# A conditioned transformer pair on one core: x loaded behind the second weight chunk and transposed one value group later

## The reference

```python
def rms_norm(x, g):
    y = x * rsqrt(mean(x * x, axis=-1) + 1e-6) * g

mod = silu(c) @ w_ada + b_ada                       # 1024 -> 3 * 1024
shift, scale, gate = split(mod, 3)
h = rms_norm(x, g_pre) * (1.0 + scale) + shift      # 512 x 1024, block 1's input
proj = h @ w_in                                     # queries, keys, values, gates of block 1
...                                                 # two attentions, output projection
x = x + gate * rms_norm(y, g_post)

mem_h = rms_norm_2(mem, mem_norm_g)                 # 256 x 1024
k, v = split(mem_h @ w_mem_kv, 2)                   # block 2's memory: keys, values
k = rms_norm_2(k per head of 256, kn_g)
...                                                 # block 2: convolution, two attentions, merge
```

## Time and profile before

| | us |
|---|---|
| runs (3): median | 1176.51 |
| lowest, highest | 1174.89, 1177.65 |
| the profiled execution: its own time | 1176.51 |
| the profiled execution: span from first to last instruction | 1174.7 |
| TensorE busy | 1141.0 |
| VectorE busy | 815.1 |
| ScalarE busy | 586.9 |
| mean granted clock of TensorE | 0.996 |

### The profile page before, as it was taken

The page is one execution under the profiler, slowest core; times in us unless marked ns, Lnnn a source line. Parts: engine busy times, 40 slices in busy tenths (PEclk is TensorE's granted clock), DMA queues, the critical chain, the costliest instruction groups (busy, mean ns, idle before and its releaser), DMA issues.

```text
span 1174.7 us, 16788 instructions
## 1 busy us (share of the span) xinstructions
PE 1141.0 (97%) x6375; PEld 948.0 (81%) x6380; DVE 815.1 (69%) x1352; ACT 586.9 (50%) x1064; POOL 64.2 (5%) x73
## 2 busy tenths in 40 slices
PE   5899999999999999999999999999999999999998
PEld 5899777766899977777777778888888888788898
DVE  5788555668575237888898885898788686853351
ACT  5663455456564455766657655324554223651320
POOL 1029400101000000000000000000000000000000
PEclk9899999999999999999999999999999999999999
DMA  9967222321454322212222143232222323223221
GB/s 343 345 223 273 91 72 73 90 63 37 148 180 157 108 72 72 72 37 90 72 90 73 36 144 126 72 108 90 90 73 84 132 81 109 97 73 108 104 85 46
DMA packets 36208, 130.41 MB, mean 111 GB/s; under 512 B 4272, under 2 KB 6576, under 8 KB 35616
## 3 DMA queue, kind: packets, MB, share of 16 engines
q1 hardware_dynamic: 32560, 112.74, 29.0%
q0 software_dynamic: 3280, 16.29, 4.2%
q10 hardware_dynamic: 288, 0.31, 0.1%
HBM read 121.72 MB, written 6.29 MB: 109 GB/s over the span
## 4 chain that ended last, share of the span: by engine, by line
PE 87%; DVE 6%; ACT 3%; issue 2%; DMA 2%; SPq 0%; POOL 0%; DVEq 0%; ACTq 0%
PE bank L463 26%; PE bank L465 25%; PE bank L464 25%; PE bank L529 2%; PE bank L677 2%; DMA raw<-in_chunks 2%; DVE wl L1760 1%; PE bank L800 1%; PE bank L705 1%; PE bank L631 1%; ACT qf L1164 1%; DVE ca L2173 1%; DVE stat L1915 0%; PE bank L807 0%; DVE cumt L2441 0%
## 5 line engine op out<-in xcount | busy, mean ns | idle before, releaser
L463 PE MATMUL bank<-hl,wh 128*128 128x512 f32 x888 | 361.7, 407 | 0.9 <-DVE u L2187 0.9
L465 PE MATMUL bank<-hh,wh 128*128 128x512 f32 x888 | 347.1, 391 | 0.0
L464 PE MATMUL bank<-hh,wl 128*128 128x512 f32 x888 | 346.2, 390 | 0.0
L1102 ACT ACTIVATE wh<-raw 128x1024 fp32r<-128x1024 f32 x185 | 191.1, 1057 | 188.9 <-PE bank L465 178.1
L1760 DVE TENSOR_TENSOR wl<-raw,wh 128x1024 fp32r<-128x1024 f32 x185 | 225.2, 1242 | 84.5 <-ACT wh L1102 84.1
L463 PEld LDWEIGHTS bank<-hl,wh 128*128 128x128 f32 x888 | 167.2, 188 | 37.9 <-issue 4.8
L465 PEld LDWEIGHTS bank<-hh,wh 128*128 128x128 f32 x888 | 166.6, 188 | 36.4
L464 PEld LDWEIGHTS bank<-hh,wl 128*128 128x128 f32 x888 | 167.3, 188 | 33.6 <-issue 3.1
L2173 DVE SCALAR_TENSOR_TENSOR ca<-u,vt,ca 128x512 f32<-128x512 f32 x232 | 157.9, 745 | 0.0
L464 PE MATMUL bank<-oh,wl 128*128 128x512 f32 (+1 forms) x256 | 93.9, 367 | 0.0
L465 PE MATMUL bank<-oh,wh 128*128 128x512 f32 (+1 forms) x256 | 93.9, 367 | 0.0
(11 more groups left out here) (323 smaller groups left out, 1676.2 us busy)
## 6 DMA issues: line engine op xcount, KB each, us to landing
raw<-in_chunks SPq DMA_DIRECT2D x193, 512.0 KB, 3.7
ada_a<-in_chunks SPq DMA_DIRECT2D x8, 512.0 KB, 10.9
ada_b<-in_chunks SPq DMA_DIRECT2D x8, 512.0 KB, 8.6
x<-in_x POOLq DMA_DIRECT2D x4, 512.0 KB, 10.5
mem_scratch<-kvm POOLq DMA_DIRECT2D x1, 2048.0 KB, 8.2
x<-in_x POOLq DMA_DIRECT2D x1, 2048.0 KB, 8.1
x_scratch<-x POOLq DMA_DIRECT2D x1, 2048.0 KB, 7.7
kvm<-mem_scratch POOLq DMA_DIRECT2D x1, 2048.0 KB, 9.5
```

Of the source, the lines that this page charges most:

```text
L463: pe.matmul(o, a[0], b[1], start=start, stop=False, **kw)
L464: pe.matmul(o, a[1], b[0], start=False, stop=False, **kw)
L465: return pe.matmul(o, a[0], b[0], start=False, stop=stop, **kw)
L1102: act.activation(wh[:, SLOT[nxt]], raw[:, RAW_SLOT[nxt]], ACT.Copy).then_inc(s.w_hi, 1)
```

## The change

Five edits, all in the first stage.

1. **Load of x.** GpSimd's queue waits until `mk1` has landed before it issues x (and the small vectors behind it).
2. **Order of pieces.** `ADA_BEHIND` puts `mk2` straight behind `mk1`, ahead of the first two ada pieces; `mk3` gets three pieces behind it. From `mk4` on the list is as before.
3. **Memory's squares.** ScalarE squares the memory's first tile only; VectorE squares and sums the second (`tensor_tensor_reduce`, with `macc` as a scratch output) ahead of its scaling of the packed vectors. A new signal, `mem_squared`, joins the two ahead of the root.
4. **x's squares and normalisation.** ScalarE squares x and takes the root at the end of head 2 and no longer ahead of head 0; the hi copy of `mk3` moves behind head 0's squares and copy. VectorE scales x into `xn` at the end of head 3, where it stood at the end of head 0.
5. **Transposes of x.** They stand ahead of value groups 1 and 2, where they stood ahead of 0 and 1.

```diff
-ADA_BEHIND = (0, 2, 1, 2, 1, 1, 1, 1, 1, 1, 1, 1, 2, 1, 0, 0, 0, 2, 0, 2, 0, 2, 0, 2)
+ADA_BEHIND = (0, 0, 2, 3, 1, 1, 1, 1, 1, 1, 1, 1, 2, 1, 0, 0, 0, 2, 0, 2, 0, 2, 0, 2)
...
             for g in range(4):
-                if g < 2:
-                    if g == 0:
+                if g in (1, 2):
+                    if g == 1:
                         pe.wait_ge(s.xn_done, 4)
-                    to_features(xn, "xT", range(4 * g, 4 * g + 4))
+                    to_features(xn, "xT", range(4 * g - 4, 4 * g))
...
         def _(pool):
+            wait_raw(pool, ("mk", 1))
             for tt in range(T):
                 pool.dma_start(x[:, tt, :], t["x"][0, tt * P:tt * P + P, :]).then_inc(s.x_in, 16)
...
-            square_rows(memx, MEM_SS, 2)
-            act.wait_ge(s.sumsq, 2)
+            square_rows(memx, MEM_SS, 1)
+            act.wait_ge(s.sumsq, 1)
+            act.wait_ge(s.mem_squared, 1)
...
-            ahead(None)
-            act.wait_ge(s.x_in, 16 * T)
-            square_rows(x, X_SS, T)
-            act.wait_ge(s.sumsq, 6)
-            act.activation(X_SS, X_SS, ACT.Sqrt, scale=1.0 / D, bias=eps6).then_inc(s.small_sqrt, 1)
+            ahead(None, 3)
...
+                if h == 0:
+                    ahead(None)
                 ahead(("mk", 2 * h + 1))
+                if h == 2:
+                    act.wait_ge(s.x_in, 16 * T)
+                    square_rows(x, X_SS, T)
+                    act.wait_ge(s.sumsq, 5)
+                    act.activation(X_SS, X_SS, ACT.Sqrt, scale=1.0 / D, bias=eps6).then_inc(s.small_sqrt, 1)
             for g in range(4):
-                if g < 2:
-                    x_copies(g)
+                if g in (1, 2):
+                    x_copies(g - 1)
...
+            dve.wait_ge(s.mem_in, 16 * 2)
+            dve.tensor_tensor_reduce(macc[:, 0, :], memx[:, 1, :], memx[:, 1, :], 1.0, 0.0, ALU.mult, ALU.add,
+                                     MEM_SS[:, 1:2]).then_inc(s.mem_squared, 1)
             dve.wait_ge(s.rows_in, 16)
...
                 ahead(("mk", 2 * h + 1))
-                if h == 0:
+                if h == 3:
                     dve.wait_ge(s.small_sqrt, 2)
                     then(dve.reciprocal(X_SS, X_SS))
```

More of the change, by code:

```diff
@@ L146 @@
     "tables_in": "masks, distances, slopes and blocks loaded",
-    "mem_in": "memory loaded", "x_in": "x loaded", "bcast_in": "lambdas and sinks loaded on every partition", "late_in": "positions, gate bias and gain",
+    "mem_in": "memory loaded", "mem_squared": "squares of the memory's second tile added up", "x_in": "x loaded", "bcast_in": "lambdas and sinks loaded on every partition", "late_in": "positions, gate bias and gain",
     "swapped": "halves of heads swapped for the rotation", "wmask_in": "banded masks of two tiles loaded", "sel_in": "rows that pick a head's bias loaded",
@@ L1079, in out_parts @@
             return [((kind, g, half), 2 * half + i, 256 * i) for i in range(2)]
-        squared_at = {name: 6 + 2 * n + 2 for n, name in enumerate(SQUARED)}
+        squared_at = {name: 5 + 2 * n + 2 for n, name in enumerate(SQUARED)}
         @block.scalar
@@ L1416, in out_squares @@
                     banks.wait_full(act, key)
-                    if squares[0] > 6:
+                    if squares[0] > 5:
                         act.wait_ge(s.sumsq, squares[0])
```

## The result

The changed kernel takes 1181.16 us (median of 5 runs, 1180.81 to 1182.37) against 1176.71 for the kernel before (median of 5, 1174.89 to 1177.84). The ratio is 1.0042, 95% interval 1.0031 to 1.0054: **4.5 us slower**. 1180.9 us had been forecast. The profiled execution took 1181.8 us, with a span of 1180.0, 5.3 more than before.

What follows compares the result with a forecast made beforehand. TensorE, busy 97% of the span, was taken as the bound. Start nothing, the 7.0 us key lead lost in x's chain: +2.1, plus +2.3 for half clock, +4.4 on 1176.51: 1180.9 us, range 1177.0 to 1184.5.

Steps and rivals of the forecast that it cites:

- Part 3: x's squares, root and scaling: chain from `mv1`'s load makes TensorE wait 8.4 us for `xn`; at full pace 2.1 us lost.
- Part 4: TensorE around the wait for `xn`: half clock costs 2.3 us, bounds 0 and 4.2.
- Part 1: Start of the first stage: gain of 0 to 3 us at first transposes, worth nothing by itself; `mk4` runs at 29.85.
- a sign of being right: TensorE's `mk4` matmuls start at 29 to 31 us and head 1's sums end near 36.5.
- a start away from 30: Sign of being wrong: `mk4` starting well away from 30 us would mean the loads don't come by bytes alone.
- Part 2: Keys on TensorE: head 1's sums end at 36.46, not 43.47, a lead of 7.0 us.
- Rival B: Wait for `xn` costs no clock, so only 2.1 us are lost: 1178.6 us; chance 0.12.
- A: At x's transposes: the lead reaches the end, `mod` 6.2 us earlier, 1170.3 us; break-even with `xn` by 56.7; chance 0.05.
- C: Half clock at both TensorE waits (`mk4`, `xn`) and through x's transposes: 2.1 + 2.1 + 4.2, 1184.9 us; chance 0.11.

Runs made afterwards that it cites:

- e2: Kernel before with edits 1 to 3 alone; x's squares, scaling and transposes left where they stood: 1177.42 us, ratio 1.0002.
- e4: Changed kernel with 32 extra unread matmuls on TensorE ahead of the wait for `xn`: 1184.82 us, ratio 1.0062.
- e5: Changed kernel with 15 extra unread matmuls on TensorE ahead of the wait for `xn`: 1179.80 us, ratio 1.0025.
- e9: The changed kernel run once more without alteration: 1181.52 us, ratio 1.0052 to the kernel before.
- e1: Changed kernel, but VectorE scales x into `xn` ahead of the lo parts of `mv2` and `mv3`: 1174.31 us, ratio 0.9977.
- e6: Changed kernel with the small vectors issued by GpSimd only after ten ada pieces: 1181.43 us, ratio 1.0036.
- e7: Changed kernel with `xn` scaled ahead of `mv2` and `mv3` and the small vectors after ten ada pieces: 1173.11 us, ratio 0.9966.

## Why the prediction was right

**The sum.** +4.4 us forecast, +4.45 measured in the medians; in the profiles `mod` is 5.5 us late, of which +4.4 was forecast, so two terms were small: x's transposes start 0.64 us later than worked out (Part 3), and the half clock costs 0.5 us more (Part 4). That the medians agree to 0.1 us is luck: the five runs of the changed kernel lie 1.6 us apart, those of the kernel before 3.0, and the two profiled executions differ by 5.3.

**Part 1, the start, worth nothing.** Right in its result (e2), wrong in its load. I took the same landing of `mk4` because the same bytes stand ahead of it. It landed at 25.4, not 27.35: the small vectors, which in the kernel before go ahead of it (DMA moved 211 GB/s in 15 to 20 us there), now came behind x and fell between `mk4` and `mk5`. DMA moved 299 GB/s in 25 to 30 us, after 391, and ScalarE's hi copy of `mk5` waited until 30.25. So `mk4`'s matmuls start at 28.73, just outside the 29 to 31 that I had named as a sign of being right: the loads don't come by bytes alone, as I had it for a start away from 30. They didn't start earlier still because VectorE took `mk4`'s lo part at 27.36, behind the three pieces that edit 2 puts behind `mk3`; the prediction has no such term. TensorE's waits for `mk3`, `mk4` and `mk5` were 0.5, 0.8 and 0.8 us, together 2.1; I had 0.6 and then 1 to 4 for `mk4` alone. By `mk5` everything had landed again (30.25 against 29.9, two loads of 1.27 behind my 27.35), so the error closed: head 1's sums ended at 36.5, as worked out, and Part 2's lead of 7.0 us stood.

**Part 3, x's chain.** Step by step, forecast and measured: `mv1` copied and x's squares begun 41.15 and 41.68 (the load 0.6 later); squares and root 6.19 and 6.30; table load to copies of head 3, 2.62 and 2.62; 1.17 and 1.17 to `mv2`'s lo part; 4.67 and 4.67 for the four instructions; 2.86 and 2.86 to the end of `xn`. x's transposes 58.8 and 59.44. The new wait 8.4 and 8.0 us, as TensorE got there 1 us later. Durations of the same instructions carried over to about a tenth; what could err were the landings. The added table load took 1.28 and the next activation stood 1.29 behind its start (47.98 to 49.27), so no drain shows here either. The Trainium skill, "ScalarE: Activation LUTs", section "What ACT_TABLE_LOAD costs", has 2.66 us for a switch, drain included; worked out from that, as an estimate, the chain would have ended 1.4 us later than it did. The measurement differs from the page here, and it decides.

**Part 4, the clock.** 2.3 forecast; 12.0 less the 9.2 of e4 is 2.8, and against e5 2.5. In e9 it was 1.9, and over the six profiles with the 8.0 us wait 2.4 in the mean. The size was right as a mean of a thing that varies. Rival B falls: the granted clock reads 0.50 in 55 to 60 us, x's transposes behind the wait took 3.68 us, and keeping TensorE busy brought them back to 1.75 (e4). "TensorE: Matmul & The Clock Gate" in the Trainium skill, in "Part 1: The HAM clock gate", gives half the clock after idling. Here the column agrees with it (0.50), unlike at the program's start.

**The rivals.** A, the lead reaching the end, needed `xn` by 56.7. e1, which had it by 50.5 (47.73 + 2.74), shows that it was there to be had: the chain that I took as given, VectorE's order, could be cut by 8 us with a move of one line. The lead from edits 4 and 5 was no illusion, only spent. C did not come: through the waits for `mk4` and `mk5`, of 0.8 us each and not 1 to 4, the granted clock stays 1.00 from 25 to 50.

**What the forecast missed.** That a shift of 2 us ahead of `mod` can be lost behind it. I said that the order behind `mod` is the same in both programs, so its start decides. The order is, the clock isn't: in e6's profiled execution the 2.7 us were taken back by rest (1111.5 against 1108.6), and even two executions of the changed kernel differ by 2.4 us there.

## What to carry to other kernels

When work is moved off the critical engine's path, follow it on every in-order engine that it crosses: here each engine had room, but x's scaling was queued behind four instructions that themselves waited for x's squares to let ScalarE go on, and TensorE stood still for 8 us. A term whose durations the trace has came out to about a tenth of a us; put the doubt into landings of loads and into the clock. And before a moved step is given up, look for where the engine that does it idles: e1 only moved x's scaling into VectorE's own idle time, and with that the change turned from a loss of 0.4% into a gain of 0.2%, 0.3% with the small vectors later. When a profile and the median disagree, look at the granted clock of every run before you blame the kernel: a profile shows one execution.

## What the runs showed of the hardware that I had not expected

- **Half clock behind short low-work stretches is a cost that moves.** Behind the wait for `xn` it cost between 1.9 and 3.0 us in six profiles with the same 8.0 us wait (`between` from 11.1 to 12.3, against 9.2 without idling), and rest varied by 3 us (1108.5 to 1111.6) with the same instructions. A wait of 2.15 us ahead of value group 1 left the granted clock at 1.00 in e1 and brought it to 0.70 in e7. Behind `mod`'s sums it stayed 1.00 in e4, where TensorE had been kept busy up to x's transposes, but read 0.72 in e5, and e4 has a stretch at 0.66 from 140 to 145 instead.
- **Small transfers hold up large ones by more than their bytes.** Five vectors spread over the partitions, 132 KB, took DMA from 391 to 299 GB/s over 5 us while its share of busy time stayed at 0.97. With them out of the way (e6) it moved 406 in the same 5 us, 0.5 MB more, and `mk5`'s hi copy started 1.7 us earlier; at 406 GB/s 132 KB are 0.3 us. The changed kernel from 20 and from 25 us, then e6 from 25 us:

```profile
20.00:25.00 5.00, 4.49 (x38) 4.29 (x37) 2.37 (x3) 2.03 (x3) 0.00 (x0) 1.00 1.04 391
25.00:30.00 5.00, 4.19 (x33) 3.77 (x32) 4.67 (x5) 1.06 (x1) 1.07 (x2) 1.00 0.97 299
...
25.00:30.00 5.00, 4.19 (x32) 3.76 (x31) 4.81 (x5) 2.23 (x3) 0.00 (x0) 1.00 1.02 406
```

- **A float32 matmul of 256 columns with plain float32 operands** takes 0.43 us at full clock (13.81 us for 32, shown as 64 instructions), 3.6 times the 0.12 of the float32r ones of the same shape.
